# Reordering the scan stage of a hybrid decoder step: state and value products, Gram products, and the place of the low-rank products among the fills

## The reference

```
def _wkv_step(S, inp):
    r, d, k, v, kk, a = inp
    s_kk = jnp.einsum('bhvk,bhk->bhv', S, kk)
    S = S * d[:, :, None, :] - s_kk[..., None] * (kk * a)[:, :, None, :] + v[..., None] * k[:, :, None, :]
    return S, jnp.einsum('bhvk,bhk->bhv', S, r)
...
g = jax.nn.sigmoid(gl) @ g2
g_a, g_b = jnp.split(jax.nn.sigmoid(u_gate), 2, axis=-1)
mixed = (g_a * (o_a.reshape(B, T, W_A) @ p_a) + g_b * (o_b @ p_b)) @ w_o
```

## Time and profile before

| quantity | value |
|---|---|
| median of 3 runs (lowest, highest) | 1652.22 us (1648.56, 1659.04) |
| profiled execution, its own time | 1651.67 us |
| its span, first to last instruction | 1649.9 us |
| PE busy in the span | 1520.4 us, 92% |
| DVE busy | 709.4 us, 43% |
| ACT busy | 351.9 us, 21% |
| POOL busy | 400.6 us, 24% |
| mean granted TensorE clock | 0.968 |

### The profile page before, as it was taken

One profiled execution on the slowest core, in us unless ns is written; L12 is line 12 of the kernel. 1 busy time (PEld: TensorE's weight loads), 2 busy tenths in 40 slices (PEclk: granted clock), 3 DMA queues, 4 the chain that ended last, 5 costly groups with the idle time before them and its releaser, 6 DMA issues. The chain is left out here.

```text
span 1649.9 us, 30005 instructions
## 1 busy us (share of the span) xinstructions
PE 1520.4 (92%) x12303; PEld 924.5 (56%) x12303; DVE 709.4 (43%) x1433; ACT 351.9 (21%) x687; POOL 400.6 (24%) x480
## 2 busy tenths in 40 slices
PE   7999998989999999898989998999999399999992
PEld 4664455554878888777778875544455233333320
DVE  4203144433255467584656553344656312222225
ACT  3002154444123323101111111121111211111122
POOL 3001056654200000107863320000411331111124
PEclk9999999999999999999999999999999599999996
DMA  6603299989432311545252224442501779999997
GB/s 231 231 34 115 84 328 337 373 328 358 126 131 81 110 54 37 118 126 143 73 147 81 78 72 169 140 170 86 220 26 39 262 257 416 386 404 405 407 349 251
DMA packets 117210, 320.96 MB, mean 195 GB/s; under 512 B 30264, under 2 KB 48120, under 8 KB 106288
## 3 DMA queue, kind: packets, MB, share of 16 engines
q1 hardware_dynamic: 89696, 244.47, 40.9%
q0 software_dynamic: 26080, 70.26, 13.2%
q10 hardware_dynamic: 1296, 4.29, 0.7%
HBM read 268.52 MB, written 58.30 MB: 198 GB/s over the span
## 5 line engine op out<-in xcount | busy, mean ns | idle before, releaser
L1209 PE MATMUL rw_pp<-rows,rw_w 128*128 128x264 f32 x960 | 218.8, 388 | 0.0
L1209 PEld LDWEIGHTS rw_pp<-rows,rw_w 128*128 128x128 f32 x960 | 182.5, 191 | 33.9 <-issue 2.8
L1613 PE MATMUL gate_p<-rows,gate_w 128*128 128x264 f32 x520 | 123.6, 390 | 9.5 <-DVE u_rw L1944 7.5
L2531 PE MATMUL x_p<-wgu,rows 128*32 128x512 f32 (+1 forms) x640 | 124.1, 611 | 2.7 <-DMA wgu<-in_we_gu 1.4
L2531 PE MATMUL x_p<-late,rows 128*32 128x512 f32 (+1 forms) x640 | 122.6, 599 | 0.0
L1613 PEld LDWEIGHTS gate_p<-rows,gate_w 128*128 128x128 f32 x520 | 97.2, 190 | 30.2 <-DVE u_rw L1944 11.3
L1568 POOL DMA_DIRECT2D t_ring<-t_blocks x128 | 69.4, 550 | 87.3 <-DVE tt L1831 79.8
L486 POOL DMA_INDIRECT rows<-in_cache_kT,page_index x41 | 41.7, 1017 | 191.0 <-PE fox_b L542 102.4
L2558 DVE SCALAR_TENSOR_TENSOR obT<-x_p,moe_ent,late 128x1024 f32<-128x1024 f32 x24 | 30.8, 1284 | 115.0 <-PE x_p L2543 115.0
L2508 POOL DMA_INDIRECT y<-obT,moe_ent x24 | 24.4, 1017 | 227.8 <-DVE obT L2558 213.1
L2549 ACT ACTIVATE rows<-h_p,vec 128x128 f32<-128x128 f32 x96 | 27.4, 367 | 245.3 <-PE h_p L2526 245.3
(11 more groups left out here) (507 smaller groups left out, 2672.7 us busy)
## 6 DMA issues: line engine op xcount, KB each, us to landing
wgu<-in_we_gu SPq DMA_DIRECT2D x16, 2048.0 KB, 17.5
late<-in_we_gu SPq DMA_DIRECT2D x16, 2048.0 KB
wd<-in_we_down SPq DMA_DIRECT2D x16, 1024.0 KB, 19.3
late<-in_we_down SPq DMA_DIRECT2D x16, 1024.0 KB
rows<-in_cache_kT SPq DMA_DIRECT2D x41, 256.0 KB
gate_w<-in_w_in SPq DMA_DIRECT2D x38, 256.0 KB, 3.0
gate_rows<-u_rw SPq DMA_DIRECT2D x72, 132.0 KB, 2.6
y<-const SPq DMA_DIRECT2D x9, 1024.0 KB, 6.3
```

The lines of the kernel that those rows point to most:

```text
L1209: mm = pe.matmul(pp[u % 2][:, c, 0:QN], w[:, n % 2, k, :] if n else e.w_first[:, k, :], e.xnT[:, k, at:at + QN], start=(i == 0), stop=(i = ...
L1613: mm = pe.matmul(bank, weights_at(pair, name)[:, k], moving[g][:, k], start=(k == 0), stop=(k == half_k - 1))
L2531: mm = pe.matmul(gu[d][at:at + n, :], hT[:, d, k, at:at + n], wgu[u][:, k, :], start=(k == 0), stop=(k == KD - 1))
```

## The change

The order inside an iteration, the list of units and the two tables that follow from it are changed. `x_from_state(c)` moves to the end of the iteration before, ahead of `corner(c)`. `x_from_values` comes ahead of `tokens`, and both Gram products come behind `u`. In the fills, gains (one in each of iterations 1 to 13) stand last, and three instead of four stand at the very start; each pair's seven products are then cut into a fill of three (i = 0, 1, 2) and one of four (i = 3 to 6), and the first fill holds 42 products and 3 gains where it held 36 and 9. `STORED` gives a gain the slot that is free behind the product ahead of it, which is slot 1 in every case. DVE leaves the add of the last product of a fill until after `update` and `add_gained` as before, but where a gain follows that product, too.

```diff
-PAIRS, NPROD, FIRST_GAINS = KD - 1, 7, 4
+PAIRS, NPROD, FIRST_GAINS = KD - 1, 7, 3
+FIRST_FILLS, LAST_FILLS = (43, 2), (1, 3)
+LONGER = tuple(range(2, NCH, 2))
+GAINED = range(1, 1 + 4 * HP - FIRST_GAINS)
+FILLS = [sum(FIRST_FILLS)] + [3 + (c in GAINED) + (c in LONGER) for c in range(1, NCH)] + [sum(LAST_FILLS)]
+FILLED = list(accumulate(FILLS))
 UNITS = [("gain", _x) for _x in range(FIRST_GAINS)]
-for _pair in range(2 * PAIRS):
-    UNITS.extend([("product", (_pair, _i)) for _i in range(NPROD)])
-    if FIRST_GAINS + _pair < 4 * HP:
-        UNITS.append(("gain", FIRST_GAINS + _pair))
+for _x in range(2 * PAIRS * NPROD):
+    if len(UNITS) + 1 in FILLED and FILLED.index(len(UNITS) + 1) in GAINED:
+        UNITS.append(("gain", FIRST_GAINS + FILLED.index(len(UNITS) + 1) - 1))
+    UNITS.append(("product", divmod(_x, NPROD)))
...
-FIRST_FILLS, LAST_FILLS = (43, 2), (1, 3)
-FILLS = [sum(FIRST_FILLS)] + [4 + (c % 3 == 0) for c in range(1, NCH)] + [sum(LAST_FILLS)]
-FIRST_ADDS = (8, 9, 9, 9, 11, 13, ...
+FIRST_ADDS = (7, 8, 8, 10, 11, 11, ...
...
-            for name in ("a21", "a22", "a11", "a12"):
+            for name in ("a11", "a21", "a22", "a12"):
...
                 if B:
-                    x_from_state(m)
+                    x_from_values(m, d)
                 if A:
                     tokens(c)
-                if B:
-                    x_from_values(m, d)
-                if A:
-                    grams(c, 0)
...
                 if B:
                     u(m, d)
                 if A:
+                    grams(c, 0)
                     grams(c, 1)
...
                 if A:
+                    x_from_state(c)
                     corner(c)
...
-                adds_upto(FILLED[c] - 1)
+                adds_upto(FILLED[c] - 1 - (c in GAINED))
```

More of the change, by code:

```diff
@@ L50 @@
 STAGED = {0: 0, 1: 2, 3: 3, 4: 1}
-STORED = [({2: 0, 4: 1, 5: 3, 6: 2}.get(_x[1]) if _kind == "product" else _x if _x < FIRST_GAINS else 1) for _kind, _x in UNITS]
-FIRST_FILLS, LAST_FILLS = (43, 2), (1, 3)
-FILLS = [sum(FIRST_FILLS)] + [4 + (c % 3 == 0) for c in range(1, NCH)] + [sum(LAST_FILLS)]
-FILLED = list(accumulate(FILLS))
-FIRST_ADDS = (8, 9, 9, 9, 11, 13, 13, 14, 15, 15, 16, 16, 17, 19, 21, 21, 21, 23, 23, 24, 24, 25, 27, 28, 29, 29, 30, 30, 31, 31, 31)
+FREE = {0: 1, 1: 1, 2: 1, 3: 0, 4: 0, 5: 0, 6: 1}
+STORED = [({2: 0, 4: 1, 5: 3, 6: 2}.get(_x[1]) if _kind == "product" else _n if _n < FIRST_GAINS else FREE[UNITS[_n - 1][1][1]])
+          for _n, (_kind, _x) in enumerate(UNITS)]
+FIRST_ADDS = (7, 8, 8, 10, 11, 11, 11, 12, 13, 14, 14, 15, 15, 18, 18, 19, 20, 20, 21, 22, 22, 24, 25, 25, 26, 27, 27, 28, 28, 28, 28)
 PLACES = [dict(a11=0, a12=1, a21=2, a22=3, s2=4, s1=5)]
```

## The result

The changed kernel takes **1635.59 us** (median of 6 runs, 1632.26 to 1637.66) against 1651.38 us (6 runs, 1648.56 to 1659.04) for the kernel before: a ratio of 0.9898, with a 95% interval of 0.9873 to 0.9922. The forecast of 1636 us was met. The profiled execution took 1635.15 us, span 1633.4 us.

What follows compares the result with a forecast made beforehand. PE was taken to bound the scan with its work unchanged, so only gaps could move: -14 + 7 - 7.5 + 2 - 3 = -15.5 us against 1651.67 us gave 1636 us, with an eight-in-ten range of 1625 to 1646.

Steps and rivals of the forecast that it cites:

- Part 1: Each iteration's waits of `tokens` for `tt`, `u` for ACT's copy and `grow` for `un` shrink: 0.93 each, 14 us less.
- Part 2: Gaps without a releaser in the small matmuls: late instruction packets grow later by 0.45 us per iteration, 7 us back.
- eleven of the fifteen iterations: Count of iterations said to show a gap without a releaser in the stretch of small matmuls.
- Both bounds: Limits of Part 2: nothing back if packets run ahead, the whole 14 us if the packet is last in every iteration.
- always last: Rival: instruction packets end every iteration's wait, so all 14 us come back; 1643 us, chance 0.23.
- near 13 us: Sign for Part 2: the "issue" idle in PE's groups of loads in the scan should sum to this.
- Part 3: Fills of iterations 1 to 15: waits for DVE and ACT go, 7.5 us less; pair 6's wide sums cost 2 more.
- Part 4: First fill: PE's gaps for DVE's adds and `t_ring` at `across(0)`, 8.2 us, become 5; 3 us less.
- the slot's store becomes the bound: Rival in the first fill: late slot stores hold adds, 3.3 us more at five seams; 1652 us, chance 0.05.
- Part 5: POOL's chain to the ring at `across(7)`: 8 us to spare become 1, no cost; up to 4 if Part 2 gives nothing.
- first rival: Instruction packets are ahead, so gaps don't grow and Part 2 is 0; 1630 us, or 1626, chance 0.27.

Runs made afterwards that it cites:

- shifted: The changed kernel with 15 repeated small products (60 instructions, 30 of them loads) on PE ahead of the first fill's first gain; 1638.56 us in one profile.
- fills_only: The changed kernel with PE's order of products within an iteration put back as before, new fills kept; 1640.09 us, ratio 0.9924 to the kernel before.
- sums_spread: The changed kernel with the second of pair 6's first two wide sums one step later; 1635.73 us, ratio 0.9919 to the kernel before.
- slots_swap: The changed kernel with two staging slots exchanged in odd pairs, so product i = 1 avoids the slot stored last; 1634.66 us, ratio 0.9908.
- spread_swap: The changed kernel with the edits of sums_spread and slots_swap together; 1635.35 us, ratio 0.9906 to the kernel before.
- fills_early1: The changed kernel with one product moved from iteration 14's fill to iteration 5's; 1635.62 us, ratio 0.9927 to the kernel before.
- order_only: The kernel before with only PE's order of products within an iteration changed, old fills kept; 1643.03 us, ratio 0.9956.
- after_again: The changed kernel run and profiled once more, nothing altered; 1635.04 us, ratio 0.9914 to the kernel before.

## Why the prediction was right, point by point

**Part 1 (14 us less): right in kind, 11 in size.** All three waits are gone, the one for `tt` too, of which I had kept 0.15 an iteration: the loads of the value product cover it. But the stretch is 5.85 us and not 5.65, so that 0.73 of the 0.93 an iteration came. The 0.2 lie in delays under 0.1 us that no releaser is named for: the value product takes 899.26 - 898.75 = 0.51 to the next load (0.42 in the earlier trace rows), and 32 Gram loads in a row 901.19 - 900.38 = 0.81 (2 x 0.36 expected).

**Part 2 (7 us back): right, 5.7.** The growth of "issue" by the removed waits was 5.8 with the old fills and 5.7 with the new, each to some 3 us. The cause, packets that come late, is shown in two ways: in `shifted` six of the ten gaps keep their instruction number while the names beside them change, and the gaps end a nearly fixed time behind a packet. The "eleven of the fifteen iterations" of the prediction are nine by the trace, counting idle of 0.15 us or more. That the lateness grows by 0.45 us in each iteration was not measured by itself; only the sum was. Both bounds fall: packets are not ahead (nothing back), nor always last (14 back). The Trainium skill's rule ("Runtime: NRT & Kernel Launch", Instruction fetch mechanics), that the sequencer's slower issue hides the fetch, does not hold in this stretch; its figure of 16 KiB for a block does. What failed is the number that I gave to look for: "near 13 us" for the sum of "issue". It is 9.3 and 8.7, because the new fills by themselves stood at 3.6 us instead of 7.9 and 6.3. They move the boundaries of packets against the stretches, which may be why, but one profile of `fills_only` does not show it. That term, some 3.5 us with the same uncertainty, I had not.

**Part 3 (7.5 less, 2 back): right.** The waits of the fills for DVE and ACT went from 9.1 and 9.4 us to 2.8 and 2.6. What stays is 1.35 us behind pair 6's first two wide sums (1.19 in the second profile), and 1.47 at 985 us in the tail, which the kernel before has too (1.47 at 1004.34). So of the 2 us given for pair 6 some 1.3 came, and nothing is seen of the third and fourth sum. `sums_spread` shows the cause of what came.

**Part 4 (3 less): the waits as forecast, the time not, 0.9 more.** The gaps behind gains went and `across(0)` finds its ring. PE's waits for DVE and the ring fell from 8.3 and 7.7 us in the two profiles to 5.4 and 4.7, which is the prediction's 8.2 to 5. Within them the slot's store, put at "about 2 us once", cost 2.87 and 3.31 us. In the kernel before DVE waited 5.47 us for such a store, and PE's longest wait was 1.3; now DVE's 6.23 us held PE for 2.87. The stores were as slow before (6.5 us for the one issued at 749.40); what changed is what stands between the store and its waiter. The mechanism is that of the rival "the slot's store becomes the bound", but its long wait stood at one seam and not at five: the changed kernel's stores issued from 697 to 742 us, at the seams before, landed within 1.7 to 4.3 us.

So these waits don't explain why the first part is no shorter. Two things that the prediction had no term for are as large. Besides the scan's start, where all four profiles have it, the clock was at 0.50 for some 3 us once in each changed profile (from 753 and from 695 us) and in neither one before; half speed for that long is worth up to 1.7 us, an estimate. And near 691 us there is a gap with no releaser, of none and 2.76 us in the two profiles before and 1.73 and 3.42 in the two after. `slots_swap` has 3.10 there, so it is not the slots'. As it varies from none to 3.5 us over all profiles, the sign of the 0.9 is open, and which of these made it is not shown.

**Part 5 (1 us to spare, no cost): half right.** In the first profile the ring of `across(7)` landed at 861.2 us, 2 us ahead of PE at 863.15, but PE had lost 2.21 us to the gap at 846.81 by then. In the second it waited 2.17 us; in `sums_spread`, `spread_swap`, `shifted` and `fills_early1` it waited 1.56 to 3.06. The margin of 8 us is used up, as worked out, and a little beyond: about 1 us is the mean of the changed kernel's two profiles. What PE gains ahead of chunk 7 beyond this, it can lose there.

The terms as measured: in the iterations -11, +5.7 - 3.5, -6.6 and +1 make -14.4 (14.2 found), with +0.9 in the first fill -13.5 (13.3 found). That the sums agree with what was found so closely says little, since the terms of "issue" rest on one profile each of `order_only` and `fills_only`. The forecast's -15.5 was made of errors that partly cancel (+3, -5, -1, +4, +1). The medians differ by 15.8 and 15.1 us in the two comparisons. The 2 us beyond the scan's own gain are not located: in the profiles the stretches outside the scan take 1 us more in the changed kernel, not less. So the mechanism of Parts 1 to 3 was right, and that the total came within 0.5 us of the forecast's 1636 was luck. One slip of the prediction changes nothing here: in its first rival, the time with all gaps of the first fill gone is 1625, not 1626.

## What to carry to other kernels

When waits are taken out of a dense run of small instructions, ask what they hid: here a third to a half of what they gave came back as instructions that arrived late. Look for idle time without a releaser inside runs of equal instructions, whether it keeps its instruction number when a few instructions are added ahead, and whether it ends a fixed time behind a packet of the instruction queue. A filler's short unit in front of a seam may be the cover of a transfer; before it is moved, read how long that transfer takes when the queues are full, not at the median.

## What the runs showed of the hardware

A gap of some 2 to 3 us on PE was at times followed by a lower granted clock, which costs again, and at times not. In the two profiles of each kernel PE's loads stood idle for 2.2 to 3.3 us eight times between 700 and 990 us. Behind two of these gaps, those of 2.87 and 2.21 us in the changed kernel's first profile, the clock fell. Behind the longest, 3.31 us up to 754.16 in `after_again`, it stayed at 1.00, and so it did behind the 2.25 and 2.41 us of the kernel before; but there it fell behind 1.67 us at 851.95. After the gap that ended at 846.81 us in the changed kernel (windows of 2 us, columns as in the earlier trace rows; then PE's loads):

```profile
845.00:847.00 2.00, 0.19 (x8) 0.19 (x11) 0.00 (x0) 0.31 (x1) 0.75 (x2) 1.00 0.87 131
847.00:849.00 2.00, 2.00 (x79) 2.00 (x76) 1.35 (x3) 0.00 (x0) 0.00 (x0) 0.81 0.85 171
849.00:851.00 2.00, 2.00 (x34) 1.88 (x31) 0.24 (x1) 0.37 (x1) 0.88 (x1) 0.50 0.11 31
851.00:853.00 2.00, 2.00 (x9) 1.61 (x9) 1.86 (x6) 0.30 (x1) 1.71 (x4) 0.84 0.23 33
...
847.99 0.82 PEld L1630 LDWEIGHTS scan_tok<-t_ring,ltm 64*64 64x64 f32 x16
...
850.64 3.89 PEld L1617 LDWEIGHTS gate_p<-rows,gate_w 128*128 128x128 f32 x16
```

The clock was 0.50 of full speed (the level of 1.2 GHz) some 2 to 4 us after the gap and back at 0.84 by 853. From `across` to the first product PE took 850.64 - 847.99 = 2.65 us; the same 48 loads take 903.67 - 902.10 = 1.57 us in the iteration shown above, so 1.1 us were lost behind a gap of 2.21, and some tenths more in the product. After the 2.87 us at 751 us the clock fell likewise, to 0.50 from 754 to 756 us. None of the prediction's terms had this.

A 132 KB store of a slot, whose median landing is 2.7 us in this kernel, took 6.9 and 6.6 us while POOL's stores of the first half's blocks ran (issued at 742.28 and 744.04). The largest of the late packets came while those of the second half ran, at 846.
